# Attention scores of two heads per key block, and decay rows read back from DRAM, in a hybrid decoder block

## What is computed

```python
def one_block(args):                       # stick-breaking attention, 8 heads of width 64
    z = jnp.einsum("bhqd,bhkd->bhqk", q_blk, k).astype(jnp.float32) * scale
    visible = (kpos[None, :] < t[:, None]) & key_valid[None, :]
    log_beta = jax.nn.log_sigmoid(z)
    log_one_minus = jnp.where(visible, jax.nn.log_sigmoid(-z), 0.0)
    log_remaining = lax.cumsum(log_one_minus, axis=3, reverse=True) - log_one_minus
    a = jnp.where(visible, jnp.exp(log_beta + log_remaining), 0.0)
    return jnp.einsum("bhqk,bhkd->bhqd", a.astype(v.dtype), v)
...
g = jnp.cumsum(chunk(g), axis=-1)          # gated delta rule, 8 heads of width 64
decay = jnp.exp(jnp.where(lower_incl, g[..., :, None] - g[..., None, :], -jnp.inf))
m = jnp.where(strict_lower, jnp.einsum("bhncd,bhnsd->bhncs", k_beta, k) * decay, 0.0)
t_inv = lax.linalg.triangular_solve(eye + m, ...)
```

## Time and profile before

| what | value |
| --- | --- |
| time, median of 3 runs | 2055.58 us (2049.75 to 2058.22) |
| profiled execution | 2049.71 us |
| its span | 2048.0 us |
| PE busy | 1920.8 us (94%) |
| DVE busy | 1372.3 us (67%) |
| ACT busy | 838.6 us (41%) |
| POOL busy | 625.7 us (31%) |
| granted TensorE clock, mean | 0.977 |

### The profile page before, as it was taken

How to read it: one execution, slowest core, us unless ns; L and a number is a source line. 1 busy time by engine, 2 the same in 40 slices (tenths; PEclk the granted TensorE clock), 3 DMA queues, 4 the chain that set the end, 5 groups by cost and what they waited for, 6 DMA issues and landing times. The chain is left out here.

```text
span 2048.0 us, 30111 instructions
## 1 busy us (share of the span) xinstructions
PE 1920.8 (94%) x11217; PEld 1697.9 (83%) x11217; DVE 1372.3 (67%) x2800; ACT 838.6 (41%) x1452; POOL 625.7 (31%) x669
## 2 busy tenths in 40 slices
PE   7989889989986999999999989999899999999999
PEld 7765666666653778899999979999899999999999
DVE  5552542532621654389899988888567777787777
ACT  4344444443452543232443346566433333333332
POOL 4123032032030100059999822222212222222221
PEclk9999999999997999999999989999999999999999
DMA  3210210210201642259999868888779999999997
GB/s 117 73 57 22 69 41 15 70 35 32 78 11 50 230 128 89 91 161 343 316 331 331 284 198 303 310 332 291 270 252 320 319 314 324 320 318 319 319 319 240
DMA packets 147985, 411.76 MB, mean 201 GB/s; under 512 B 15616, under 2 KB 63872, under 8 KB 147328
## 3 DMA queue, kind: packets, MB, share of 16 engines
q1 hardware_dynamic: 109056, 269.31, 37.9%
q0 software_dynamic: 38784, 140.53, 21.0%
HBM read 360.23 MB, written 49.55 MB: 200 GB/s over the span
## 5 line engine op out<-in xcount | busy, mean ns | idle before, releaser
L1491 ACT ACTIVATE expert_hi<-raw 128x1024 fp32r<-128x1024 f32 x288 | 305.5, 1061 | 422.1 <-PE psE L86 406.3
L1646 DVE TENSOR_TENSOR expert_lo<-raw,expert_hi 128x1024 fp32r<-128x1024 f32 x215 | 263.0, 1224 | 148.0 <-ACT expert_hi L1491 147.1
L84 PE MATMUL psE<-w_hi,expert_hi 128*128 128x384 f32 x1024 | 351.3, 343 | 10.0 <-DVE expert_lo L1646 5.5
L84 PE MATMUL psE<-x2h,expert_hi 128*128 128x384 f32 x1024 | 349.6, 341 | 8.6 <-POOL expert_lo L1610 6.9
L85 PE MATMUL psE<-x2l,expert_hi 128*128 128x384 f32 x1024 | 344.9, 337 | 0.0
L86 PE MATMUL psE<-x2h,expert_lo 128*128 128x384 f32 x1024 | 344.9, 337 | 0.0
L86 PE MATMUL psE<-w_hi,expert_lo 128*128 128x384 f32 x1024 | 344.3, 336 | 0.0
L85 PE MATMUL psE<-w_lo,expert_hi 128*128 128x384 f32 x1024 | 344.0, 336 | 0.0
L1604 POOL DMA_INDIRECT few_gathered<-in_peer_v,picked_expert x128 | 133.6, 1043 | 428.5 <-DVE few_y L1837 388.1
L1604 POOL DMA_INDIRECT few_gathered<-in_peer_u_rows,picked_expert x128 | 152.6, 1192 | 250.2 <-DVE few_gathered L1830 224.1
L1610 POOL TENSOR_TENSOR expert_lo<-raw,expert_hi 128x1024 fp32r<-128x1024 f32 x73 | 186.3, 2552 | 132.7 <-ACT expert_hi L1491 131.1
(11 more groups left out here) (317 smaller groups left out, 3380.3 us busy)
## 6 DMA issues: line engine op xcount, KB each, us to landing
raw<-in_peer_u SPq DMA_DIRECT2D x128, 512.0 KB, 4.8
raw<-in_peer_v SPq DMA_DIRECT2D x128, 512.0 KB, 6.6
expert_acts<-gelu SPq DMA_DIRECT2D x124, 192.0 KB, 5.3
gelu<-expert_acts SPq DMA_DIRECT2D x124, 192.0 KB, 3.8
expert_gates<-shared SPq DMA_DIRECT2D x4, 4096.0 KB, 15.8
gates_in<-expert_gates SPq DMA_DIRECT2D x32, 512.0 KB, 6.2
ring<-in_w_xonly SPq DMA_DIRECT2D x24, 512.0 KB, 3.3
ring<-in_w_full SPq DMA_DIRECT2D x16, 512.0 KB, 3.8
```

The lines of the kernel that those rows point to most:

```text
L84: nc.tensor.matmul(out, sh, mh, start=first, stop=False)
L1491: nc.scalar.activation(wh[:, s % R, :], raw[:, s % R, :], ACT.Copy).then_inc(S["hi_done"], 1)
L1646: v.tensor_tensor(wl[:, s % R, :], raw[:, s % R, :], wh[:, s % R, :].bitcast(F32), ALU.subtract).then_inc(S["lo_done"], 1)
```

## The change

Three edits, made together.

1. The attention steps are ordered by key block first, with the two heads of a block next to each other. A "z" unit now issues the scores of both heads (banks 0 and 1), a "cum" unit both exponents. There are 5 rounds of level, cum, products, z, soft, soft. ACT does the six activations of a z unit, three for each head, in one go. The running sum is kept per head and updated in place. The fill steps that stood after a cum now stand ahead of and after each z: the chunk dv ends at z 2, the chunk z at z 4.
2. The products of values take turns between the heads within each key block.
3. The rows of decays and beta no longer come from PE. Ahead of the pairs, two transposes and one copy put them on 40 partitions, five transfers from POOL's queue write them to DRAM, and for each pair one transfer (from POOL's queue too) reads two heads' rows back, repeated on all 128 partitions. DVE and ACT then read `rows_all` in SBUF. PE's transposes no longer wait for the decays.

```diff
-ATT = [(e, kb) for e in range(2) for kb in range(NT, -1, -1)]
+ATT = [(e, kb) for kb in range(NT, -1, -1) for e in range(2)]
...
-UNITS = [("z", 0), ("z", 1), ("soft", 0)]
-for _a in range(len(ATT)):
-    UNITS += [("products" if _a % 2 else "level", _a // 2 + 1), ("cum", _a)]
-    UNITS += [("z", _a + 2)] if _a + 2 < len(ATT) else []
-    UNITS += [("soft", _a + 1)] if _a + 1 < len(ATT) else []
+UNITS = [("z", 0), ("soft", 0), ("soft", 1)]
+for _j in range(NT + 1):
+    UNITS += [("level", _j + 1), ("cum", _j), ("products", _j + 1)]
+    UNITS += [("z", _j + 1), ("soft", 2 * _j + 2), ("soft", 2 * _j + 3)] if _j < NT else []
...
-            room += [(("unit", u), 1 if unit == "cum" and UNITS[u + 1][0] == "z" else 0)]
+            room += [(("unit", u), 1 if "z" in (unit, UNITS[min(u + 1, len(UNITS) - 1)][0]) and u else 0)]
...
+            def load_rows(i):
+                if i:
+                    pool.wait_ge(S["decay_beta"], PER["decay_beta"] * i)
+                    pool.wait_ge(S["row_exp"], PER["row_exp"] * i)
+                source = rows_dram[:, 2 * i:2 * i + 2, :].rearrange("k (a e) t -> a k e t", a=1)
+                pool.dma_start(rows_all[:, :, :, :], source.broadcast_to([P, 2, 2, TOK])).then_inc(rows_loaded, 16)
+
+            pool.wait_ge(S["rows_copied"], 1)
+            for n in range(NT + 1):
+                lo_col, hi_col = tile_cols(n)
+                pool.dma_start(rows_dram[:, :, lo_col:hi_col].rearrange("k h t -> h k t"),
+                               row_heads[n * HEADS:(n + 1) * HEADS, :, 0:hi_col - lo_col]).then_inc(rows_stored, 16)
+            pool.wait_ge(rows_stored, 16 * (NT + 1))
+            load_rows(0)
...
@@ ScalarE, ahead of the decays of a pair
+                act.wait_ge(rows_loaded, 16 * (i + 1))
+                for e in range(2):
+                    h = slice(e * HD, (e + 1) * HD)
+                    last = nc.scalar.activation(egr[h, 1:, :], rows_all[h, 0, e, META:].rearrange("p (n t) -> p n t", t=P),
+                                                ACT.Exp)
+                inc(last, "row_exp")
...
@@ ScalarE, units
                     elif unit == "z":
+                        for k in (2 * a, 2 * a + 1):
+                            e, kb = ATT[k]
...
+                            wait("z_scores", k + 1)
+                            turn.then(nc.scalar.activation(part, bank[0:r, e, q0:], ACT.Abs))
+                            turn.then(nc.scalar.activation(part, part, ACT.Exp, scale=-1.0))
+                            inc(nc.scalar.activation(part, part, ACT.Ln, bias=c["ones"][0:r, 0:1]), "z_ln")
...
@@ VectorE
+                dve.wait_ge(rows_loaded, 16 * (i + 1))
                 grow_rows(0)
                 grow_rows(1)
...
@@ TensorE, decays and transposes of a pair
-                wait("rows_ready", 1)
-
-                wait("logs", 2)
-                grow(0)
-                grow(1)
                 fill("grow1")
...
                 for n in range(2, NT + 1):
-                    grow(n)
                     fill(f"grow{n}")
                 wait("qk_ready", 1)
                 wait("silued", 3)
-                wait("decay_beta", 3)
...
@@ TensorE, units
+                        wait(*(("att_exp", 2 * a) if a else ("att_inputs", 1)))
+                        for e in range(2):
+                            inc(mm(bank[0:r, e, q0:], kn[half(e), lo:hi], qn[half(e), q0:], start=True, stop=False,
+                                   skip_group_check=True), "z_scores")
...
+                        for kb in range(2) if a == 0 else range(2, NT + 1):
                             r, q0 = tile_rows(kb), first_query(kb)
+                            for e in range(2):
+                                last = mm(bank[half(e), 0, q0:], v[0:r, kb, i * P + e * HD:i * P + (e + 1) * HD],
+                                          a_[0:r, e, A_OFF[kb]:A_OFF[kb] + SEQ - q0], start=kb == 0, stop=kb == NT)
```

More of the change, by code:

```diff
@@ L500, in _ @@
[L500 to L509, removed]
-                        wait("att_exp", a + 1)
-                        part = a_[:, e, A_OFF[kb]:A_OFF[kb] + P]
-                        inc(nc.gpsimd.affine_select(out=part, in_=part, compare_op=ALU.is_gt, fill=0.0, base=0,
-                                                    pattern=[[1, P]], channel_multiplier=-1), "att_masked")
+                    if unit == "cum" and a < NT:
+                        for e in range(2):
+                            kb = NT - a
+                            q0 = first_query(kb)
+                            wait("cumulated", 2 * a + e + 1)
+                            wait("z_masked", 2 * a + e + 1)
+                            if kb < NT:
+                                nc.gpsimd.tensor_tensor(acc[:, e, q0 + P:], acc[:, e, q0 + P:], sp_[:, e, q0 + P:], ALU.add)
+                            inc(nc.gpsimd.tensor_copy(acc[:, e, q0:q0 + P], sp_[:, e, q0:q0 + P]), "later_ready")
+                        for e in range(2):
+                            wait("att_exp", 2 * a + e + 1)
+                            part = a_[:, e, A_OFF[kb]:A_OFF[kb] + P]
+                            inc(nc.gpsimd.affine_select(out=part, in_=part, compare_op=ALU.is_gt, fill=0.0, base=0,
+                                                        pattern=[[1, P]], channel_multiplier=-1), "att_masked")
@@ L1077, in square_sums @@
                     inc(last, "norm_sums")
-                def grow(n):
-                    r = tile_rows(n)
-                    if n >= 3:
-                        wait("decay_beta", n - 2)
-                    inc(mm(bank[:, grow_bank(n), 0:4 * r].rearrange("p (k c) -> p k c", k=4), c["ones"][0:r, :],
-                           rows_in[0:r, n, :, 0:r], start=True, stop=True), "grown")
                 fill("start")
@@ new lines, in _ @@
+                        lo, hi = tile_cols(NT - a)
+                        r, q0 = tile_rows(NT - a), first_query(NT - a)
+                        wait(*(("att_exp", 2 * a) if a else ("att_inputs", 1)))
+                        for e in range(2):
+                            inc(mm(bank[0:r, e, q0:], kn[half(e), lo:hi], qn[half(e), q0:], start=True, stop=False,
+                                   skip_group_check=True), "z_scores")
+                    elif unit == "cum":
+                        for k in (2 * a, 2 * a + 1):
+                            e, kb = ATT[k]
+                            r, q0 = tile_rows(kb), first_query(kb)
+                            if kb:
+                                wait("z_masked", k + 1)
+                            else:
+                                wait("z_soft", k + 1)
+                            last = mm(bank[0:r, e, q0:], c["neglow"][0:r, 0:r], sp_[0:r, e, q0:], start=False,
+                                      stop=kb == NT, skip_group_check=True)
+                            if kb < NT:
+                                later = q0 + P if kb else 0
+                                wait("later_ready", k - 1)
+                                last = mm(bank[0:r, e, later:], c["negones"][:, 0:r], acc[:, e, later:],
+                                          start=False, stop=True, skip_group_check=True)
+                            inc(last, "cumulated")
+                    elif unit == "pv":
+                        if a == 0:
+                            wait("att_exp", len(ATT))
+                            wait("att_masked", len(DIAG))
+                        for kb in range(2) if a == 0 else range(2, NT + 1):
@@ L1221, in _ @@
                             r, q0 = tile_rows(kb), first_query(kb)
-                            last = mm(bank[half(e), 0, q0:], v[0:r, kb, i * P + e * HD:i * P + (e + 1) * HD],
-                                      a_[0:r, e, A_OFF[kb]:A_OFF[kb] + SEQ - q0], start=kb == 0, stop=kb == NT)
-                        if e == 1:
+                            for e in range(2):
+                                last = mm(bank[half(e), 0, q0:], v[0:r, kb, i * P + e * HD:i * P + (e + 1) * HD],
+                                          a_[0:r, e, A_OFF[kb]:A_OFF[kb] + SEQ - q0], start=kb == 0, stop=kb == NT)
```

107 lines of the change are left out of this document (39 added, 68 removed).

## The result

The kernel after took 2076.59 us (median of 13 runs, 2064.73 to 2084.61), the kernel before 2058.19 beside it (13 runs, 2048.04 to 2064.43). The ratio is 1.0091, with a 95% interval of 1.0069 to 1.0113: slower by 14 to 23 us. The forecast was 2060, that is +4.8 us and no change; the rival that the clock stays low had 2072.

What follows compares the result with a forecast made beforehand. PE was taken to set the time, busy 129.4 of 143.6 us a pair but not at full clock. -16 - 12.8 - 5.7 + 0.3 + 36 + 3 = +4.8 us: 2054.5, or 2060 on the median; range 2044 to 2076.

Steps and rivals of the forecast that it cites:

- the clock stays low: Rival: PE in the second half of the units loses 4 us more in each of three pairs; 2072 us, chance 0.23.
- The overlap of two heads: Scores and products of values on PE: the second head's scores cost nothing, gaining 16 us; values in turns gain 12.8.
- that rival: Rival: the heads overlap only in part, scores and values bring 21 us instead of 29; 2068 us, chance 0.05.
- The rows through DRAM: Ahead of the pairs: 0.3 us for two small transposes, transfers hidden; rival of rows coming late 2070 us, chance 0.04.
- The grow products: PE's grow products gone: 1.2 us gained in each of pairs 0 to 2, 2 in pair 3, 5.7 in all.
- the loss of clock that follows such a spell stays: Behind the transposes: PE's idle spell grows from 2.1 to over 4 us, with the clock loss behind it unchanged.
- Six activations in one go: ACT's hi stands behind both heads' activations where chunks end: 12.0 us a pair, 36 for pairs 0 to 2; pair 3 +3.
- end of dv: Where chunk dv ends, after z 2: PE idles 5.5 us instead of 1.86, +3.7 a pair.
- end of z: Where chunk z ends, after z 4: PE idles 6.3 us instead of 0.91, +5.4 a pair.
- level 4: Third tile of level 4 waits for ACT's copy of the first: PE idles 1.8 us, +1.5 a pair.
- The end of z will now cost that too: +1.7: Behind the end of z: a stretch of 3.4 us at clock 0.50, 1.7 us of PE's work lost a pair.
- Pair 3: Last pair, nothing to fill with: PE idles 2.3, 3.9 and 3.9 us in levels 3 to 5; +3, between 0 and 7.

Runs made afterwards that it cites:

- the values alone: The kernel before with only the products of values in turns between the heads: 2046.89 us, ratio 0.996 to before.
- The part alone: The kernel before with only the rows of decays through DRAM, grow products gone: 2057.63 us, ratio 1.0005 to before.
- the fillers: Unread products in PE's idle spells, ratios to before: kernel after 0.9925; kernel before 0.992; before with only rows through DRAM, behind the transposes only, 0.9956.

## Why the prediction was wrong, step by step

**The overlap of two heads** held in both places. Scores 1.06 us against 1.05 by the forecast; values 3.29 us less in pair 1 (6.59 to 3.30) against 3.2, and -13.2 us of front for the values alone, against -12.8. (The forecast used 3.2 for what is saved in its sum and for what is left in its signs; by the sum 3.4 would be left.) The Trainium skill, "TensorE: Matmul & The Clock Gate", section on measured speedup, lists less than full overlap for three and four tiles. With the two tiles of this kernel the trace shows full overlap at 512 columns, so the measurement decides, and that rival falls.

**The rows through DRAM** came in time. Up to 700 us neither ACT nor DVE waits for them; ACT's first use in pair 0 stands in its queue without a wait:

```profile
103.00 1.26 ACT L616 ACTIVATE exp_g_row<-rows_all 64x512 f32<-64x512 f32 x2
```

**The grow products.** The wait was foreseen ("over 4 us", 3.87 measured) and so was what ends it. In pair 1 the norm's product and the next chunk's step are 29.11 us apart (231.99 to 261.10); before it was 28.92 (227.82 to 256.74), with 1.46 us of the same wait ahead of the norm but no fall of the clock. That fall costs 1.5 us: from the norm's product to the fourth product of the fill steps 3.15 us pass (231.99 to 235.14), where it was 1.66 (227.82 to 229.48). Without it the chain gained 1.3 us, against 1.2 (by the forecast's own terms, 0.52 and 0.6, it is 1.1, and its 5.7 is 5.4). What was wrong is the half sentence that "the loss of clock that follows such a spell stays". It holds for the stretch right behind the wait, 3.4 us before (256.70 to 260.10) and after (262.60 to 266.00), but not for what comes later: with that wait filled in after, the next stretch was half as long. The part alone gained 2.2 us of front, not 5.4, and nothing in time; the fillers show that its wait costs clock, but not that the missing 3.2 us are just that.

**Six activations in one go.** The mechanism and the sizes of its waits were right:

| place | forecast idle | measured | forecast z to next step | measured |
| --- | --- | --- | --- | --- |
| end of dv | 5.5 | 5.20 | 8.0 | 7.83 |
| end of z | 6.3 | 5.87 | 8.9 | 8.67 |
| level 4 | 1.8 | 1.47 | | |

ACT's timeline of after, pair 1, shows hi directly behind the second head's Ln, 3.17 us after the first Abs; DVE's has the soft between lo and take.

```profile
304.83 0.49 ACT L676 ACTIVATE decays<-psB 128x384 f32<-128x384 f32 x1 [3.53 <-PE psB L1189]
...
307.48 0.61 ACT L678 ACTIVATE decays<-decays,ones 128x384 f32<-128x384 f32 x1
308.00 1.04 ACT L520 ACTIVATE ring_h<-ring 128x1024 fp32r<-128x1024 f32 x1
```

The same moment in DVE's timeline:

```profile
309.08 1.23 DVE L713 TENSOR_TENSOR ring_l<-ring,ring_h 128x1024 fp32r<-128x1024 f32 x1 [5.43 <-ACT ring_h L520]
310.33 0.56 DVE L957 SCALAR_TENSOR_TENSOR conv_work<-psB,decays 128x384 f32<-128x384 f32 x1
310.81 0.70 DVE L725 TENSOR_TENSOR proj<-psB,rstd 128x528 f32<-128x528 f32 x1
```

**The clock: the step that failed.** The prediction put "The end of z will now cost that too: +1.7", one more stretch of 3.4 us in each pair. What came was 17.1 us more at 1.2 GHz in each of pairs 1 and 2 (27.3 against 10.2). PE was busy for 12.8 us more of it (23.0 against 10.2), and work that takes 0.42 to 0.43 us there takes 0.24 at full clock, so 44% is lost: 5.6 us a pair, 3.9 more than counted. The waits were 0.3 + 0.4 + 0.3 = 1.0 us shorter than forecast. That leaves 2.9, and the pairs missed by that: with 12.0 - 3.9 - 3.2 - 1.2 = +3.7 expected in pairs 1 and 2, they came out at +6.7 and +6.5. (The forecast's bound of 9 a pair "without the clock" is 10.3 by its own terms.) The fillers say nearly the same: they took 8.6 us off pair 1 of after (150.3 to 141.7) and 3.8 off pair 1 of before (143.6 to 139.8), so the clock costs 4.8 us a pair more in after, where the forecast counted 1.7. The Trainium skill, "TensorE: Matmul & The Clock Gate", section on HAM oscillation, counts the loss as half of the throttled time; by an estimate from that, the 17.1 us here would cost 8.6, more than the pairs show. PE was busy for 12.8 of those 17.1 us.

**Pair 3** missed by the same amount in another place: 3 - 3.9 - 3.2 - 2 = -6.1 expected, -3.1 measured. Its mean clock fell from 0.92 to 0.90, and its waits were those forecast (3.6 us the longest for y, against 3.9). **Pair 0** came out at +4.2, where +4.0 was expected, although its mean clock was 0.92 instead of 0.96 there too; what made up for it was not traced. Over the pairs the misses are 0.2, 3.0, 2.8 and 3.0 us, 9 of the 9.6 by which front missed. The times lie 19 us apart by the ratio and front 14.4; no run shows where the other 4 lie.

So the forecast of the waits was right, its clock term of 1.7 us a pair was too small by about 3, and the rival "the clock stays low" decided. I had given it 0.23 and named as its condition that the work between two idle spells doesn't bring the clock back. That was not quite it: between the spells the clock did come back each time. What grew in pairs 1 and 2 was the number of falls (5 a pair instead of 3) and the length of three of them. The evidence against it that I quoted, the single drop of 3.4 us behind 1.86 us of idling, said nothing on idle spells three times as long.

## What to carry to other kernels

Where PE is the bound and its clock is not full, count each idle spell twice: once for its length, and once for the work behind it that may run at half speed; here the second count made a loss of a change that costs nothing in sum at full clock. A merged step that makes an engine's burst longer (six activations in one go) delays whatever was queued behind that burst: move the short instruction that feeds the bound engine ahead of it, which here turned a loss of 0.9% into a gain of 1.3%. Idle spells that can't be removed can be filled with products that nothing reads: in three kernels with many spells of 1 to 6 us, fillers at most of them took 15 to 34 us off `front`.

## What the runs showed of the hardware that was not expected

- The same wait can drop the clock or not. At the norm of pair 0, PE waited 1.46 us before and 1.45 us after, behind the same instructions. Before, the fill steps behind it ran at full speed, as the timeline of PE shows:

```profile
227.82 1.12 PE L1277 MATMUL psB<-norm_work,blocks 128*128 128x512 f32 x2 [1.46 <-ACT norm_work L697]
...
229.48 0.39 PE L84 MATMUL psB<-xh,ring_h 128*128 128x512 f32 x1
```

After, the same fourth product starts 1.5 us later behind the norm:

```profile
231.99 2.08 PE L1269 MATMUL psB<-norm_work,blocks 128*128 128x512 f32 x2 [1.45 <-ACT norm_work L698]
...
235.14 0.46 PE L84 MATMUL psB<-xh,ring_h 128*128 128x512 f32 x1
```

What decides between the two was not tried.

- Filling one wait shortened the low stretch behind the next one, from 6.9 to 3.4 us, although that wait kept its 2.64 us.
- `back`, the same in every kernel, took 1397 to 1413 us in the profiled executions. What makes it vary was not tried.
